# First layer's input projection on one core: block one in fp32, blocks two to four as three products of rounded and remaining parts

## What is computed

```python
def even_mixer(hn, p, ctx, layer_idx):
    proj = hn @ p['w_in']
    qa, ka, va, q_down, ckv, kpe = jnp.split(
        proj, [HA * 2 * DA, 2 * HA * 2 * DA, A_COLS, A_COLS + Q_LORA, A_COLS + Q_LORA + KV_LORA], axis=-1)
    ...
    qb = heads(rmsnorm(q_down, p['q_norm']) @ p['w_uq'], HB)
    ckv = rmsnorm(ckv, p['kv_norm'])
    ...
```

## Time and profile before

| what | value |
|---|---|
| median of three runs | 2282.62 us |
| the runs | 2278.49, 2282.62, 2282.74 us |
| the profiled execution | 2279.34 us, of which 2277.6 us are the span of the instructions |
| TensorE busy | 2123.2 us, 93% of the span |
| VectorE busy | 1083.3 us, 48% |
| ScalarE busy | 650.0 us, 29% |
| GpSimd busy | 152.0 us, 7% |
| mean granted TensorE clock | 0.953 |
| HBM | 71 GB/s over the span |

### The profile page before, as it was taken

How to read it: one execution, slowest core, us unless ns; L and a number is a source line. 1 busy time by engine, 2 the same in 40 slices (tenths; PEclk the granted TensorE clock), 3 DMA queues, 4 the chain that set the end, 5 groups by cost and what they waited for, 6 DMA issues and landing times.

```text
span 2277.6 us, 41041 instructions
## 1 busy us (share of the span) xinstructions
PE 2123.2 (93%) x18328; PEld 1772.4 (78%) x18328; DVE 1083.3 (48%) x1922; ACT 650.0 (29%) x1152; POOL 152.0 (7%) x145
## 2 busy tenths in 40 slices
PE   6998999998999999989998779999979899999997
PEld 3544444558999999979995368888845799999997
DVE  3015645326555563243634656767642555555422
ACT  2001433213333342132334433333111333333211
POOL 1000000000000000000002622222000000000000
PEclk8998999999999999989998879999969999999998
DMA  9022543612222212222120000000021222221122
GB/s 321 26 74 77 193 148 139 231 37 74 75 75 75 75 52 77 77 68 75 56 65 8 19 2 4 3 3 4 4 79 38 69 79 77 75 75 52 53 76 72
DMA packets 141408, 163.71 MB, mean 72 GB/s; under 512 B 2369, under 2 KB 106865, under 8 KB 141233
## 3 DMA queue, kind: packets, MB, share of 16 engines
q1 hardware_dynamic: 137872, 148.81, 20.3%
q0 software_dynamic: 3360, 12.28, 1.5%
HBM read 157.32 MB, written 3.75 MB: 71 GB/s over the span
## 4 chain that ended last, share of the span: by engine, by line
PE 85%; DVE 10%; ACT 2%; DMA 1%; issue 1%; POOL 0%; ACTq 0%; DVEq 0%; SPq 0%; POOLq 0%
PE ps L218 81%; DMA ring<-in_ada_w 1%; DVE work L386 1%; PE ps L314 1%; ACT work L1463 1%; PE ps L846 1%; DVE x_lo_r L399 1%; DVE work L1939 1%; PE ps L329 1%; DVE work L1502 1%; DVE work L1984 0%; DVE work L387 0%; PE ps L1698 0%; PE ps L1716 0%; DVE work L1975 0%
## 5 line engine op out<-in xcount | busy, mean ns | idle before, releaser
L218 PE MATMUL ps<-x_hi_r,w_lo 128*128 128x320 f32 x2080 | 476.7, 311 | 0.0
L218 PE MATMUL ps<-work 64*64 64x64 f32 (+6 forms) x4942 | 386.4, 271 | 32.3 <-ACT work L1859 9.1
L218 PE MATMUL ps<-x_hi_r,w_hi 128*128 128x320 f32 x1664 | 382.8, 311 | 11.0 <-DVE x_lo_r L399 11.0
L218 PE MATMUL ps<-x_lo_r,w_hi 128*128 128x320 f32 x1664 | 382.4, 311 | 8.2 <-DVE g_lo L561 8.2
L218 PEld LDWEIGHTS ps<-work 64*64 64x64 f32 (+4 forms) x4942 | 248.3, 149 | 159.6 <-issue 102.5
L218 PEld LDWEIGHTS ps<-x_hi_r,w_lo 128*128 128x128 f32 x2080 | 349.3, 188 | 0.9
L218 PEld LDWEIGHTS ps<-x_hi_r,w_hi 128*128 128x128 f32 x1664 | 278.8, 189 | 14.5 <-issue 8.6
L218 PEld LDWEIGHTS ps<-x_lo_r,w_hi 128*128 128x128 f32 x1664 | 281.3, 190 | 8.8 <-DVE g_lo L561 8.8
L440 DVE SCALAR_TENSOR_TENSOR work<-ps,par,work 128x511 f32<-128x511 f32 (+1 forms) x188 | 103.4, 550 | 284.4 <-ACT work L537 276.7
L487 DVE TENSOR_TENSOR w_lo<-ring,w_hi 128x1024 fp32r<-128x1024 f32 (+1 forms) x152 | 158.3, 1076 | 98.2 <-ACT w_hi L476 98.2
L537 ACT ACTIVATE work<-ps,par 128x640 f32<-128x640 f32 x88 | 77.8, 884 | 415.9 <-PE ps L218 415.9
(11 more groups left out here) (321 smaller groups left out, 2324.4 us busy)
## 6 DMA issues: line engine op xcount, KB each, us to landing
ring<-in_ada_w SPq DMA_DIRECT2D x24, 2048.0 KB, 8.0
ring<-in_ffn_up SPq DMA_DIRECT2D x44, 1024.0 KB, 6.7
ring<-in_ffn_down SPq DMA_DIRECT2D x16, 1408.0 KB, 7.0
ring<-in_l_w_in SPq DMA_DIRECT2D x11, 1024.0 KB, 5.2
ring<-in_l_w_out SPq DMA_DIRECT2D x4, 2048.0 KB, 9.0
ring<-in_l_w_in SPq DMA_DIRECT2D x3, 2048.0 KB, 8.2
h<-in_xT POOLq DMA_DIRECT2D x1, 2560.0 KB, 14.7
out_yT<-work POOLq DMA_DIRECT2D x4, 640.0 KB, 3.9
```

The source lines that it names most:

```text
L218: return pe.matmul(out, lhsT, rhs, start=first, stop=last)
```

## The change

Block one (queries) stays as it was. Meanwhile ScalarE copies the eight tiles of hn, rounded, into xh over `merged` (waiting for them by `hn_ready`, which both halves of a tile now raise), and after its first and second eviction copies the weights of block two, rounded, in four parts into free work memory (`m0_w_hi`). VectorE subtracts them from the ring slot in place (`m0_w_lo`), then waits for the four product groups of block one, and makes xl over hn, tile by tile. Blocks two and three go through `project_split`; block four has three products of 512 columns in each k step, x stationary. The weights of block three are rounded after the evictions of groups 4 and 5, those of block four after those of groups 8 and 9 (counted from 0). Since a split group's halves lie elsewhere in their PSUM pair, evictions read `spair`. As `merged` now holds xh, the ckv rows are evicted straight to their two places in `ckv_b`; squares and scaling go over these two pieces, and the two closing copies are gone. Counters of later stages get offsets. Left out of the diff are four places that only add such an offset to a wait on `x_lo`, `in_lo` or `in_hi`.

```diff
--- before.py
+++ after.py
@@ -362,7 +362,7 @@
                         act.activation(xh(t, 0, NL), hn(t, 0, NL), ACT.Identity, bias=shift(t, 0))
                         act.activation(xh(t, NL, NT), hn(t, NL, NT), ACT.Identity, bias=shift(t, 1)).then_inc(sg("x_hi"), 1)
                         continue
-                    act.activation(hn(t, 0, NL), hn(t, 0, NL), ACT.Identity, bias=shift(t, 0)).then_inc(sg("hn_half"), 1)
+                    act.activation(hn(t, 0, NL), hn(t, 0, NL), ACT.Identity, bias=shift(t, 0)).then_inc(sg("hn_ready"), 1)
                     act.activation(hn(t, NL, NT), hn(t, NL, NT), ACT.Identity, bias=shift(t, 1)).then_inc(sg("hn_ready"), 1)
 
         def norm_sum(pe, n):
@@ -394,7 +394,7 @@
 
         def norm_lo(dve, t, shift, layer):
 
-            dve.wait_ge(sg("x_hi"), KT * layer + t + 1)
+            dve.wait_ge(sg("x_hi"), KT + KT * layer + t + 1)
             for c, (a, b) in enumerate(SEG):
                 ins = dve.scalar_tensor_tensor(xl(t, a, b), hn(t, a, b), shift(t, c), xh(t, a, b).bitcast(F32),
                                                ALU.add, ALU.subtract)
...
@@ -604,8 +604,10 @@
                 for src, kk, *gain in items[k][0]:
                     if c >= 2:
                         act.wait_ge(sg("st_sum"), c - 1)
-                    act.activation(sqb[0:kk, (c % 2) * NT:(c % 2) * NT + NT], src, ACT.Square, scale=gain[0] if gain else 1.0)\
-                        .then_inc(sg("st_sq"), 1)
+                    for piece, a, b in src.pieces if src is ckv_new else ((src, 0, NT),):
+                        ins = act.activation(sqb[0:kk, (c % 2) * NT + a:(c % 2) * NT + b], piece, ACT.Square,
+                                             scale=gain[0] if gain else 1.0)
+                    ins.then_inc(sg("st_sq"), 1)
                     c += 1
                 return c
 
@@ -660,7 +662,9 @@
                     rep(k + 1)
                 dve.wait_ge(sg("st_turned"), i0 + k + 1)
                 for j, (out, in_, gain, kk) in enumerate(outs):
-                    ins = dve.scalar_tensor_tensor(out, in_, gain, pair_ap(pairs[k % len(pairs)], 0, NT, 0, kk), ALU.mult, ALU.mult)
+                    for piece, a, b in out.pieces if out is ckv_new else ((None, 0, NT),):
+                        ins = dve.scalar_tensor_tensor(out if piece is None else piece, in_ if piece is None else piece, gain,
+                                                       pair_ap(pairs[k % len(pairs)], a, b, 0, kk), ALU.mult, ALU.mult)
                     if j == len(outs) - 1:
                         ins.then_inc(sg("st_used"), 1)
                     else:
@@ -696,29 +700,65 @@
 
         V0 = 12
 
+
+
+        m0_block = [i for i, b in enumerate(blocks) if b[0] == "win"][:4]
+        m0_w = lambda j: KT * (blocks[m0_block[j]][1][0][4])
+        M0W = W0 + 4 * NT + 4 * NK + 6 * 512
+        m0_hi = [None, rounded("m0_w1", "work", M0W + 4096, 4096), rounded("m0_w2", "work", M0W, 2816),
+                 rounded("m0_w3", "work", M0W + 2816, 4096)]
+        m0_lo = lambda j: wl_b[:, SLOT * (m0_block[j] % RING):SLOT * (m0_block[j] % RING) + m0_w(j)]
+        m0_k3 = lambda b: b.rearrange("p (k c) -> p k c", k=KT)
+
+        def m0_w_hi(act, j, part):
+            i, w = m0_block[j], m0_w(j) // 4
+            if part == 0:
+                act.wait_ge(full[i % RING], 16 * parts_before[i % RING][i + 1])
+                if j >= 2:
+                    act.wait_ge(*released[m0_block[j - 2]])
+                if j == 3:
+                    act.wait_ge(*released[m0_block[1]])
+            at = SLOT * (i % RING) + w * part
+            act.activation(m0_hi[j][:, w * part:w * part + w], ring[:, at:at + w], ACT.Copy).then_inc(sg("in_hi"), 1)
+
+        def m0_w_lo(dve, j, part):
+            w = m0_w(j) // 4
+            dve.wait_ge(sg("in_hi"), 4 * (j - 1) + part + 1)
+            at = SLOT * (m0_block[j] % RING) + w * part
+            dve.tensor_tensor(wl_b[:, at:at + w], ring[:, at:at + w], m0_hi[j][:, w * part:w * part + w].bitcast(F32),
+                              ALU.subtract).then_inc(sg("in_lo"), 1)
+
         def mix0_pe(pe):
             n = 0
-            for part in range(2):
-                w = next_block(pe)
-                for m in range(4):
-                    if n >= 3:
-                        pe.wait_ge(sg("m0_copied"), n - 2)
-                    x_ready = (lambda k: pe.wait_ge(sg("hn_ready"), k + 1)) if n == 0 else None
-                    project(pe, n % 3, lambda k: w[:, k, P * m:P * m + P], hn, KT, before=x_ready)\
+            w = next_block(pe)
+            for m in range(4):
+                if n >= 3:
+                    pe.wait_ge(sg("m0_copied"), n - 2)
+                x_ready = (lambda k: pe.wait_ge(sg("hn_ready"), 2 * k + 2)) if n == 0 else None
+                project(pe, n % 3, lambda k: w[:, k, P * m:P * m + P], hn, KT, before=x_ready)\
+                    .then_inc(sg("m0_prod"), 1)
+                n += 1
+            released.append((sg("m0_prod"), n))
+            for j, cuts in ((1, [(P * m, P * m + P) for m in range(4)]), (2, ((0, 128), (128, 192), (192, 320), (256, 352)))):
+                next_block(pe)
+                pe.wait_ge(sg("in_lo"), 4 * j)
+                wh, wl = m0_k3(m0_hi[j][:, :]), m0_k3(m0_lo(j))
+                for c0, c1 in cuts:
+                    pe.wait_ge(sg("m0_copied"), n - 2)
+                    x_ready = (lambda k: pe.wait_ge(sg("x_lo"), k + 1)) if n == 4 else None
+                    project_split(pe, n % 3, lambda k: wh[:, k, c0:c1], lambda k: wl[:, k, c0:c1], xh, xl, KT, x_ready, c1 - c0)\
                         .then_inc(sg("m0_prod"), 1)
                     n += 1
                 released.append((sg("m0_prod"), n))
-            w = next_block(pe)
-            for c0, c1 in ((0, 128), (128, 192), (192, 320), (256, 352)):
-                pe.wait_ge(sg("m0_copied"), n - 2)
-                project(pe, n % 3, lambda k: w[:, k, c0:c1], hn, KT, p1=c1 - c0).then_inc(sg("m0_prod"), 1)
-                n += 1
-            released.append((sg("m0_prod"), n))
-            w = next_block(pe)
+            next_block(pe)
+            pe.wait_ge(sg("in_lo"), 12)
+            wh, wl = m0_k3(m0_hi[3][:, :]), m0_k3(m0_lo(3))
             for tt in range(5):
                 pe.wait_ge(sg("m0_copied"), n - 2)
                 for k in range(KT):
-                    ins = mm(pe, bank(2 * (n % 3)), hn(k, P * tt, P * tt + P), w[:, k, :], k == 0, k == KT - 1)
+                    for x, w in ((xh, wh), (xl, wh), (xh, wl)):
+                        ins = mm(pe, bank(2 * (n % 3)), x(k, P * tt, P * tt + P), w[:, k, :], k == 0 and x is xh and w is wh,
+                                 k == KT - 1 and w is wl)
                 ins.then_inc(sg("m0_prod"), 1)
                 n += 1
                 if tt == 0:
@@ -739,36 +779,53 @@
             pe.wait_ge(sg("lam_prod"), 1)
             mm(pe, bank(6, 2), ones[0:64, :], small[0:64, 26:28]).then_inc(sg("lam_sum"), 1)
 
+
+        class TwoPieces:
+            pieces = ((ckv_b[:, 0:NL], 0, NL), (ckv_b[:, KP0:NK], NL, NT))
+        ckv_new = TwoPieces()
+
         low_norms = plan_stats([
             ([(tile(qd_b, 0), P), (qd_b[0:64, NT:2 * NT], 64)], ones[:, 0:1], 1.0 / QL, 16,
              [(tile(qd_b, 0), tile(qd_b, 0), pc("q_norm", 0), P),
               (qd_b[0:64, NT:2 * NT], qd_b[0:64, NT:2 * NT], pc("q_norm", 1, 1, 0, 64), 64)]),
-            ([(sqb[:, 0:NT] if False else merged(0), P)], ones[:, 0:1], 1.0 / KVL, 16,
-             [(merged(0), merged(0), pc("kv_norm"), P)])])
+            ([(ckv_new, P)], ones[:, 0:1], 1.0 / KVL, 16,
+             [(ckv_new, ckv_new, pc("kv_norm"), P)])])
 
         def mix0_act(act):
             n = 0
+            for t in range(KT):
+                act.wait_ge(sg("hn_ready"), 2 * t + 2)
+                act.activation(xh(t), hn(t), ACT.Copy).then_inc(sg("x_hi"), 1)
             for m in range(8):
                 act.wait_ge(sg("m0_prod"), n + 1)
+                psum = lambda a, b: pair_ap(n % 3, a, b) if m < 4 else spair(n % 3, a, b)
                 if m < 4:
-                    act.activation(q(m), pair_ap(n % 3), ACT.Copy, scale=DA ** -0.5).then_inc(sg("m0_copied"), 1)
+                    act.activation(q(m), psum(0, NT), ACT.Copy, scale=DA ** -0.5).then_inc(sg("m0_copied"), 1)
                 else:
-                    act.activation(kk_(m - 4, 0, NL), pair_ap(n % 3, 0, NL), ACT.Copy)
-                    act.activation(kk_(m - 4, KP0, NK), pair_ap(n % 3, NL, NT), ACT.Copy).then_inc(sg("m0_copied"), 1)
+                    act.activation(kk_(m - 4, 0, NL), psum(0, NL), ACT.Copy)
+                    act.activation(kk_(m - 4, KP0, NK), psum(NL, NT), ACT.Copy).then_inc(sg("m0_copied"), 1)
                 n += 1
+                if m in (0, 1, 4, 5):
+                    for part in range(2 * (m % 2), 2 * (m % 2) + 2):
+                        m0_w_hi(act, 1 + m // 4, part)
             for i in range(4):
```

(34 more changed lines are left out.)

## The result

Over 20 runs each, the changed kernel's median is 2272.45 us and that of the kernel before 2291.03. The ratio is 0.9928, with a 95% interval of 0.9904 to 0.9952: 16.5 us less, between 11 and 22. The ratio leaves out two runs of the kernel before, of 5674 and 7924 us, and three of the changed kernel, of 2294 to 2301 us at a granted clock of 0.931 to 0.934; with these three the gain, mean against mean, is 12.4 us instead of 16.4. The forecast's gain of 19.85 lies in the interval; its range for the time, 2255 to 2268 around 2261.0, does not hold the median. The profiled execution has a span of 2269.5 us, 8.1 less than the one of before.

A forecast was written before the change was run, and what follows sets the result against it. The prediction took the projection to be bound by TensorE's products alone. It summed 13.17 + 7.15 + 0.73 - 1.2 = 19.85 us gained, which from a mean of 2280.8 gave 2261.0 us, range 2255 to 2268.

The forecast's parts named there:

- Split groups: Blocks two and three: eight fp32 groups of 8.69 us become split groups of 7.04 us, 13.17 us gained.
- Value tiles: Block four: five tiles go from 6.87 to 5.44 us each, 7.15 us gained (bounds 6.2 to 8.8).
- The bounds' middle: Block four: a rounded 512-column product costs 227 ns, between bounds of 213 and 235 ns.
- the dear wide product: Rival in block four: a rounded 512-column product holds the array 0.63 us, 28.6 us slower overall, 2309; chance 0.03.
- the bare stream time: Rival in block four: 213 ns a product, the V block gives 8.8 instead of 7.15 us, 2259.4; chance 0.12.
- New wait: After block one's fourth group: TensorE waits for the first x_lo tile only, 1.2 us lost (bounds 0.8 to 2).
- Cover: Weight rounding and subtraction for blocks two to four finish about 10 us before needed and cost nothing.
- Tail: End of the projection stage: two copies leave before the lambda product's operand, 0.73 us gained.
- Stage: The changed projection stage: all terms summed, 19.85 us gained.
- all later stages as long as before: Behind the projection: later stages keep their lengths and start 20 us sooner.
- the clock as a rival: Clock falls after the new stall, 2 to 4 us lost, chance 0.10; or tail gives 2 to 3 back, chance 0.07.
- The base: Whole kernel before the change: 2280.8 us, the mean of four executions, from which the gain was taken.

The follow-up runs named there:

- x_lo_early: The changed kernel, but VectorE makes each x_lo tile once the fourth group of block one has read that tile of hn; ratio 0.9933 (0.9905 to 0.9961).

## Why the prediction was right in its sum and wrong in its time

- **Split groups.** 13.17 less 1.2 forecast, 69.49 - 57.53 = 11.96 measured. Narrow weights made no difference, as said.
- **Value tiles.** 5.44 forecast, 5.47 measured. The bounds' middle, from the scan's pair and from the 320-column pitch plus 192 columns, was right. So the dear wide product, the bare stream time (213 ns) and the Trainium skill's 216 ns ("TensorE: Matmul & The Clock Gate", "Back-to-back issue gap") all fall: the trace has 228 ns.
- **New wait.** 1.2 forecast, 1.24 measured by the evictions (8.28 - 7.04), and x_lo_early without the wait has 7.03; VectorE's eight tiles took 5.97 us, and TensorE waited once.
- **Cover.** No wait on w_lo. Block four's weights landed at 120.1, forecast 121, and its products began at 139.
- **Tail.** 0.73 forecast; TensorE's wait went from 3.19 to 2.47.
- **Stage.** 19.85 forecast, 18.26 in the profile, 19.83 and 19.88 where the clock did not stay down longer behind the statistics.
- **The step that failed** is "all later stages as long as before". I named the clock as a rival, but only for falls after the new wait and at the tail, at 2 to 4 us. I had one profile, in which attention had 10 us at half clock, and took its length for the kernel's own. The same program took 106 and 121 us there in two profiles, the changed kernel 116.6 in both of its own, and the other kernels 107 to 122. Which execution gets which falls stays open.
- **The base** failed with it. I took 2280.8 from four executions, 4 us apart, and called that their scatter. Over 20 the median is 2291.03; the first four, 2278 to 2283, were by their times all executions with a short attention, which was luck: in the later comparisons 50 of 119 runs of that kernel took under 2284 us. Of the 11.4 us between forecast and median, 10.2 are this and 1.2 the gain (18.6 between the medians). Since the runs of the kernel before lie in two groups, its median is coarse; without the two runs over 5000 us it is 2285.43 and the mean 2287.5. By the means of the runs that the ratio keeps, the base was 6.7 us off and the gain 3.5.

The section "HAM oscillation — how this bites in real kernels" of the Trainium skill's page "TensorE: Matmul & The Clock Gate" tells how waits of TensorE bring the clock down. The trace agrees in that at the tail of the kernel before the clock was 0.52 over the 10.7 us from the lambda operand on, right behind a wait of 3.19 us. No forecast of attention's time follows from it: at 203 us in the changed kernel the clock fell though TensorE had been busy 3.68 of 4.00 us.

## What to carry to other kernels

Price a product by its pitch at the moving width in use, from the same kernel, and waits by the dependence's first tile only; each term of the stage held here to 0.15 us. Before predicting a whole time, see whether its runs fall in several groups and whether the profile shows a stage with thin products and falls of the granted clock: such a stage can give or take most of what the change is worth (15 us here, against 19.9) from one execution to the next. Judge a change upstream of it by its own stage, and the whole by many runs.

## What was unexpected of the hardware

The first head group of attention, with the same work on all engines, took from 106.0 to 122.0 us without an edit inside it. In the two profiles of one program 14.6 of 15.0 us of difference stand in TensorE's busy time, at granted clocks of 0.95 and 0.83. Once down, the clock stayed at 1.2 GHz for 27 us in the changed kernel with TensorE busy 27.21 of 27.30 us, while behind the statistics it came back after 10 to 14. A rounded product of 512 columns costs 228 ns from start to start and one of 320 costs 147. The 192 further columns thus cost 81 ns, one column in each cycle of 2.4 GHz, and by that estimate either product has 13 to 15 ns besides.
